# A Strassen feed-forward on one core: eight early pairs in place of four, spills issued by ACT, gate parts three units ahead, down groups of 4, 5 and 6

## The reference, cut to what matters

```
mix = concat([attn, rec]) @ w_out
h = h + rmsnorm(mix, g_post_mix)
u = rmsnorm(h, g_pre_ffn)
f = square(relu(u @ w_ff1)) @ w_ff2        # 1024 -> 4096 -> 1024, 1024 tokens, fp32
h = h + rmsnorm(f, g_post_ffn)
```

## Time and profile before

| | us |
|---|---|
| median of three runs | 2499.36 |
| their range | 2497.77 to 2503.22 |
| the profiled execution | 2501.51 |
| its span, first to last instruction | 2499.5 |
| busy: PE, DVE, ACT, POOL | 2311.5, 1553.2, 1016.2, 557.3 |
| last part of the program: first early unit starts | 1784.8 |
| last down unit starts its last matmul | 2443.9 |

### The profile page before, as it was taken

One profiled execution on the slowest core, in us unless ns is written; L12 is line 12 of the kernel. 1 busy time (PEld: TensorE's weight loads), 2 busy tenths in 40 slices (PEclk: granted clock), 3 DMA queues, 4 the chain that ended last, 5 costly groups with the idle time before them and its releaser, 6 DMA issues. The chain is left out here.

```text
span 2499.5 us, 30965 instructions
## 1 busy us (share of the span) xinstructions
PE 2311.5 (92%) x11293; PEld 1951.4 (78%) x11293; DVE 1553.2 (62%) x2437; ACT 1016.2 (41%) x1688; POOL 557.3 (22%) x467
## 2 busy tenths in 40 slices
PE   8989699989999999999999989789979998899986
PEld 5779588877888888888887988667758887688765
DVE  7699666665643444433444685472898776567787
ACT  5478545453421111111112663474543333454431
POOL 2021222214322222222221211003301221120332
PEclk9975599999999999999999999899989999899998
DMA  9024100014211111111110011002334445553521
GB/s 364 18 85 154 50 14 13 23 44 143 85 34 51 51 51 50 50 37 47 50 50 26 35 34 34 18 1 93 130 123 177 185 169 199 209 185 112 175 68 68
DMA packets 66289, 219.06 MB, mean 88 GB/s; under 512 B 8160, under 2 KB 12416, under 8 KB 63744
## 3 DMA queue, kind: packets, MB, share of 16 engines
q1 hardware_dynamic: 66176, 217.59, 24.9%
HBM read 174.04 MB, written 43.52 MB: 87 GB/s over the span
## 5 line engine op out<-in xcount | busy, mean ns | idle before, releaser
L158 PE MATMUL set<-gate_hi,w_hi 128*128 128x512 f32 x420 | 169.0, 402 | 26.4 <-DVE gate_lo L2329 23.3
L1948 ACT CAST w_hi<-w_raw 128x512 fp32r<-128x512 f32 x152 | 94.4, 622 | 230.0 <-PE set L160 80.3
L1647 POOL TENSOR_TENSOR w_lo<-w_raw,w_hi 128x512 fp32r<-128x512 f32 x64 | 87.3, 1366 | 426.9 <-ACT w_hi L1948 426.8
L158 PE MATMUL set<-b_hi,w_hi 128*128 128x512 f32 x416 | 164.3, 395 | 19.2 <-DVE w_lo L2241 19.2
L159 PE MATMUL set<-gate_lo,w_hi 128*128 128x512 f32 x420 | 167.6, 399 | 0.0
L160 PE MATMUL set<-gate_hi,w_lo 128*128 128x512 f32 x420 | 167.3, 398 | 0.0
L3359 DVE TENSOR_SCALAR work<-work,vec 128x1024 f32<-128x1024 f32 x22 | 17.9, 814 | 236.0 <-ACT work L3089 228.9
L159 PE MATMUL set<-b_lo,w_hi 128*128 128x512 f32 x416 | 163.3, 393 | 0.0
L160 PE MATMUL set<-b_hi,w_lo 128*128 128x512 f32 x416 | 163.3, 393 | 0.0
L3381 DVE SCALAR_TENSOR_TENSOR x<-down,mod,x 128x512 f32<-128x512 f32 x160 | 120.0, 750 | 66.4 <-PE down L160 64.4
L2329 DVE TENSOR_TENSOR gate_lo<-gate_raw,gate_hi 128x512 fp32r<-128x512 f32 x105 | 100.3, 957 | 60.0 <-ACT gate_hi L2006 60.0
(11 more groups left out here) (567 smaller groups left out, 6474.2 us busy)
## 6 DMA issues: line engine op xcount, KB each, us to landing
gates<-x SPq DMA_DIRECT2D x16, 2048.0 KB, 7.3
gate_raw<-gates SPq DMA_DIRECT2D x105, 256.0 KB, 2.8
w_raw<-in_w_ff SPq DMA_DIRECT2D x47, 512.0 KB, 5.9
ada<-in_ada_w SPq DMA_DIRECT2D x32, 512.0 KB, 3.3
work<-in_f_w_u SPq DMA_DIRECT2D x22, 512.0 KB, 3.3
work<-in_f_w_v SPq DMA_DIRECT2D x22, 512.0 KB, 3.4
work<-in_f_w_out SPq DMA_DIRECT2D x22, 512.0 KB, 4.3
down_raw<-in_w_ff SPq DMA_DIRECT2D x18, 512.0 KB, 5.3
```

Of the source, the lines that this page charges most:

```text
L158: nc.tensor.matmul(out, w_hi, x_hi, start=start, stop=False)
L1647: nc.gpsimd.tensor_tensor(lo[:, :], source(n), f32(hi[:, :]), ALU.subtract).then_inc(pool_lo, 1)
L1948: nc.scalar.copy(w_parts(n)[0][:, :], source(n)).then_inc(w_hi_s, 1)
```

## The change

`EARLY` is 8: P1 and P2 of eight pairs are done ahead of the rest. Their results have no room in SBUF all at once beside the squares of h, so SP stores each early P2 to DRAM (`keep_p2`) and loads it straight into block 0 of its gate buffer when that buffer is free (`bring_p2`). The scratch tiles for u2, y and P1 become blocks 5, 7 and 6 of the gate buffer. The store of a gate buffer is issued by ACT (`spill`), as two transfers, 256 KB and 1.5 MB (block 1 is left out for pairs under `LAST`; of pair 15 only four blocks go out, and its block sums are not made). SP no longer waits for block sums. The down groups have 4, 5 and 6 pairs; there are four gate_hi and gate_lo buffers, made three units ahead. DVE's order in the down stage is sum (n+3), gate_lo (n+3), w_lo (n+2). The low parts for the 16th pair are made by DVE instead of POOL. The low parts of raw weights (P1, P2, P4) stay on POOL.

```diff
-EARLY, GROUP = 4, 5
+EARLY = 8
+SIZES = (4, 5, 6)
...
-        raws = raw + [at(f"down_raw{i}", SLOT(i), [P, 2, KT * P]) for i in range(3)]
+        raws = raw + [at(f"down_raw{i}", SLOT(s), [P, 2, KT * P]) for i, s in enumerate((0, 1, 2, 13))]
...
-        early_p = [[work[:, 2 * x + i, 0:512] for i in range(2)] for x in range(EARLY)]
-        u2, y = work[:, 6, 512:1024], work[:, 7, 512:1024]
-        own_p1 = [work[:, 2 + i, 512:1024] for i in range(2)]
+        early_p1 = [work[:, x, 0:512] for x in range(EARLY)]
+        early_p2 = [work[:, x, 512:1024] for x in range(EARLY)]
...
+        EARLY_AT = ((0, 0), (0, 0), (0, 1), (1, 0), (1, 1), (0, 0), (0, 1), (1, 0))
...
+                    if i == P1:
+                        sp.wait_ge(spilled[(w - PAIRS) % 2], 16 * SPILLS * ((w - PAIRS) // 2 + 1))
...
+                def keep_p2(x):
+                    sp.wait_ge(p_s, 2 * x + 2)
+                    sp.dma_start(d["p2_keep"][x], early_p2[x]).then_inc(p2_kept[x], 16)
+
+                def bring_p2(x):
+                    if x >= 2:
+                        sp.wait_ge(spilled[x % 2], 16 * SPILLS * (x // 2))
+                    sp.dma_start(blk(x, 0), d["p2_keep"][x]).then_inc(p2_back[x % 2], 16)
...
+                sp.wait_ge(pool_lo, units.low[9])
+                load_up(1, 1)
+                sp.wait_ge(pool_lo, units.low[11])
+                load_up(0, 0)
+                for x in range(3, 6):
+                    keep_p2(x)
+                sp.wait_ge(pool_lo, units.low[13])
+                load_up(0, 1)
+                sp.wait_ge(pool_lo, units.low[15])
+                load_up(1, 0)
+                for x in range(6, EARLY):
+                    keep_p2(x)
+                sp.wait_ge(kept, 16 * KT)
+                sp.wait_ge(h_squared, N)
+                sp.wait_ge(t_hi_s, 5 * HALF)
+                sp.wait_ge(t_lo_s, 4 * HALF)
+                bring_p2(0)
+                bring_p2(1)
                 for x in range(PAIRS):
                     if x == LAST:
                         sp.wait_ge(done, units.at[(x, P1)] + 1)
-                        for j in (2, 3):
-                            load_down(j, 0)
-                            load_down(j, 1)
+                        load_down(0, 2, 0)
+                        load_down(0, 3, 0)
                         sp.wait_ge(done, units.at[(x, P2)] + 1)
-                        load_down(4, 0)
-                        load_down(4, 1)
                         for b in range(4):
                             load_gate(b)
+                        load_down(0, 2, 1)
+                        load_down(0, 3, 1)
+                        load_down(1, 4, 0)
+                        load_down(1, 4, 1)
                     sp.wait_ge(dve_lo, units.low[units.at[(x, P3)]])
...
-                    sp.wait_ge(t_s, 4 * x + 4)
-                    sp.dma_start(d["gates"][x], gates[x % 2]).then_inc(spilled[x % 2], 16)
-                sp.wait_ge(done, UP)
-                sp.dma_start(end_o_raw[:, 0, :], d["w_ff2"][2 * LAST]).then_inc(end_o_loaded, 16)
-                sp.dma_start(end_o_raw[:, 1, :], d["w_ff2"][2 * LAST + 1]).then_inc(end_o_loaded, 16)
+                    if 1 <= x < EARLY - 1:
+                        bring_p2(x + 1)
...
                 def early_out(n):
+                    x, i = units.all[n]
                     act.wait_ge(done, n + 1)
-                    act.wait_ge(h_added, 7)
-                    nc.scalar.copy(early_p[n // 2][n % 2], bank(n)).then_inc(p_s, 1)
+                    if i == P1:
+                        act.wait_ge(h_added, 7)
+                        nc.scalar.copy(early_p1[x], bank(n)).then_inc(p_s, 1)
+                    else:
+                        act.wait_ge(h_s, h_count(x))
+                        nc.scalar.copy(early_p2[x], bank(n)).then_inc(p_s, 1)
...
                 def square_h(k):
+                    act.wait_ge(p2_kept[k], 16)
                     nc.scalar.activation(work[:, k, span[1]], tok(k, span[1]), ACT.Square).then_inc(h_squared, 1)
 
                 def copy_p1(x):
                     act.wait_ge(done, units.at[(x, P1)] + 1)
-                    act.wait_ge(h_total, 2)
-                    if x >= EARLY + 2:
-                        act.wait_ge(u2_s, x - 1)
-                    nc.scalar.copy(own_p1[x % 2], A_BANK).then_inc(p_s, 1)
+                    act.wait_ge(spilled[x % 2], 16 * SPILLS * (x // 2))
+                    nc.scalar.copy(p1_at(x), A_BANK).then_inc(p_s, 1)
...
+                def spill(x):
+                    if x < LAST:
+                        act.wait_ge(t_s, 4 * x + 4)
+                        act.dma_start(d["gates"][x][:, 0:512], blk(x, 0)).then_inc(spilled[x % 2], 16)
+                        act.dma_start(d["gates"][x][:, 1024:4096], gates[x % 2][:, 1024:4096])\
+                            .then_inc(spilled[x % 2], 16)
...
+                    act.wait_ge(done, UP + b - 3)
+                    nc.scalar.copy(gate_hi[b % 4][:, :], gate_raw[b % 4][:, :]).then_inc(gate_hi_s, 1)
...
+                def out11(x):
+                    if x < EARLY:
+                        dve.wait_ge(p2_back[x % 2], 16 * (x // 2 + 1))
+                        nc.vector.tensor_tensor(blk(x, 0), p1_at(x), blk(x, 0), ALU.add).then_inc(c11_s, 1)
+                    else:
+                        dve.wait_ge(done, units.at[(x, P2)] + 1)
+                        dve.wait_ge(spilled[x % 2], 16 * SPILLS * (x // 2))
+                        dve.wait_ge(p_s, EARLY + x + 1)
+                        nc.vector.tensor_tensor(blk(x, 0), B_BANK, p1_at(x), ALU.add).then_inc(c11_s, 1)
...
+                def end_weights_low(h):
+                    dve.wait_ge(end_o_hi_s, h + 1)
+                    nc.vector.tensor_tensor(end_o_lo[h][:, :], end_o_raw[h], f32(end_o_hi[h][:, :]), ALU.subtract)\
+                        .then_inc(end_o_lo_s, 1)
+
+                def end_gate_low(j):
+                    dve.wait_ge(end_g_hi_s, j + 1)
+                    nc.vector.tensor_tensor(g_lo[j][:, :], end_g_raw[:, j, :], f32(g_hi[j][:, :]), ALU.subtract)\
+                        .then_inc(end_g_lo_s, 1)
...
+                    if n + 2 < UP:
                         if not units.on_pool(n + 2):
                             weights_low(n + 2)
-                        if n + 2 >= UP:
-                            gate_low(n + 2 - UP)
-                    if n + 3 < ALL and not units.on_pool(n + 3):
-                        weights_sum(n + 3)
+                        if n + 3 in units.combined:
+                            weights_sum(n + 3)
+                        if n + 3 == UP:
+                            gate_low(0)
+                    else:
+                        if n + 3 in units.combined:
+                            weights_sum(n + 3)
+                        if n + 3 < ALL:
+                            gate_low(n + 3 - UP)
+                        if n + 2 < ALL and not units.on_pool(n + 2):
+                            weights_low(n + 2)
```

370 lines of the change are left out of this document (199 added, 171 removed).

## The result

The changed kernel takes 2464.8 us (median of 4 runs, 2463.9 to 2466.7) beside 2501.3 (2497.8 to 2503.4) for the kernel before on the same chip: a ratio of 0.9856, interval 0.9839 to 0.9874. The time lies in the predicted range, 15 us above the predicted 2450. One execution of the kernel with four edits (4222.0) and one of before beside it (3286.5) ran far slower than all others of the same kernels, at a lower granted clock, and the ratios leave both out (the median of 2446.5 is 2446.3 without it). The profiled execution has a span of 2461.8; the span fell by 37.7 us, where 50.9 were summed up.

The account below looks back on a forecast made before the run. PE was taken as the bound, interrupted by DVE or what DVE waits for. Gains of 14.0 (up stage), 21.7 (turn) and 15.2 (groups) sum to 50.9, span 2448.6; with 1.5 for small waits 2450 us, range 2439 to 2471.

Parts of the forecast that it names:

- What bounds the kernel: Whole kernel: PE is the bound, interrupted by DVE or what DVE waits for; 24.1, 22.2 and 18.4 us lost at three places.
- Start of the up stage: First up units: PE waits 4.1 us for sum_h(0) and the parts behind it, plus half clock; 7.1 lost instead of 24.1.
- the early units end at 1809.2 + 21.8 = 1831.0: Before the up stage: eight more early units give PE 21.8 us of work, ending at 1831.0.
- Pairs 0 to 7: Up stage: a closed round of spill and fetch takes 14.1 us against PE's 13.6; price 3, bounds 0 and 9.
- Rival 2: Up stage: the spill and fetch round is longer, 17.7 us, costing 22 instead of 3; 2469, 18 %.
- The turn: From up to down stage: earlier gate requests hide the DMA; price 0.5, bounds 0 and 6, 21.7 us gained.
- seven units, 19 us, from there to its use: Down stage: lead of gate 13 behind 5 MB, which take at most 18.3 us; hidden, but by little.
- rival 3: Turn's pause moves to gate 13 or group 2's weights: 5 with its half clock, 8 in all; 2458 to 2462, 12 %.
- The groups: Down stage: new DVE order removes the 0.74 waits and absorbs 2.28 sums; 3.2 lost of 18.4, 15.2 us gained.
- plus six POOL w_lo that lock it out for 1.1 each: Last group's end: POOL's low parts delay DVE, bringing its work to 35.8 us against 32.6 of PE.
- Rival 4: 16th pair on DVE: the end list slips, PE pauses above 3 us twice, final sums start 4 later; 2460, 10 %.
- The other rivals: Besides the summed case (50 %): less cost than charged, 2440, 5 %; slower through copy_p1 waiting for spills, 2500 to 2515, 3 %.

Follow-up runs that it names:

- the kernel with four edits: Changed kernel with sum_h(0) after eight early units, last-group P4 low parts on DVE, x's refill spread, two w_hi ahead of ACT's t4 casts: 2446.5 us, ratio 0.9789.
- the refill spread: Changed kernel with x's eight transfers and two weight loads sent one behind each of gates 12 to 21, not all ahead of gate 13: 2459.6 us, ratio 0.9833.
- the spills on SP: Changed kernel with SP instead of ACT issuing the gate-block spills of pairs 0 to 14: 2468.7 us, ratio 0.9873.

## Why the prediction was right in kind and too high in gain

The figures in brackets are the losses that the prediction left at each place.

**What bounds the kernel**: right. Each of the four pauses is one of PE waiting for DVE, for what DVE holds up, or for what DVE itself waits for. What made the kernel faster is shown in part. Undone one by one, the order and lead of the gate parts cost 9.7 us, the spills on ACT's queue 7.8 and the group sizes nothing. `EARLY` = 4 and the old order of loads at the turn were not put back; that they are behind the 9.1 of the up stage and most of the rest is read from positions.

**Start of the up stage** (7.1 left): the step "the early units end at 1809.2 + 21.8 = 1831.0" failed. They end at 1836.1, by the first pause, 5.9 us. It took POOL's operations beside DVE as a cost to DVE; what a full DVE does to POOL had no price. The text had named the place ("ACT's list there is nearly full"), not priced it. The rest held: sum_h binds, the pause is 4.04 beside 4.1, the half clock 2.6 beside 2.7, h_total released DVE at 1836.9.

**Pairs 0 to 7** (3 left): right in kind, a little high. Spills start at 1867.87, 1881.62, 1895.38, 1909.14, 1922.89 and 1937.83: 13.75 apart (once 14.94), where the round was put at 14.1 and DVE at 13.8. DVE's own 13.8 is what was measured; the round doesn't bind. The 1.5 MB took 5.8, the rest of the spill lay beside it, where 6.4 were taken. Two waits, 0.77 and 1.04, are what came of it, about 2. Rival 2 (the longer round) fell, and the spills on SP showed that one queue would not have brought it either.

**The turn** (0.5 left): the 21.7 came but for 4.1. The price of the transfer held: from 2124.94 the 5 MB and gate 13 took 16.8 us, at most 18.3 were said. What failed is the lead, "seven units, 19 us, from there to its use". On DVE w_lo of the unit before stands behind gate_lo of gate 13, and PE wanted it at 2140.9, 15.9 after the issue. This was rival 3, below its price of 8, and the refill spread shows it.

**The groups** (3.2 left): the small waits are gone as costed, but the fourth pause is 6.8. The step "plus six POOL w_lo that lock it out for 1.1 each", with 1.0 for a wait "at the last P4 unit", failed: in the stretch that made the fourth pause, 2377.96 to 2386.40, DVE was not locked out at all; POOL was, for 8.4 us. (Behind the pause DVE lost some: gate_lo took 1.37 at 2394.14 and 1.78 at 2397.63 instead of 0.69, where no wait of PE above 0.25 came of it.) The rows of before had shown both sides, the join of 3.36 and the 3.02 that PE waited for POOL; only the first was carried over.

So + 5.9 - 0.5 - 1 + 4.1 + 5 = 13.5 of the 50.9, and 37.4 are left; measured are 36.9, and 0.8 more by which this execution reached the stage earlier. That the time lies in the range owes something to the range's width: three steps failed the same way, and no rival had their sum. Rival 4 came in place, a pause above 3 us in the last group, but not in cause. The other rivals didn't come: no copy_p1 made anyone wait, and the final sums start no later.

## What to carry to other kernels

Where two engines hold each other up, as POOL and DVE do here, ask not only how much the slower one delays the faster, but whether the faster one ever stops: beside a list without gaps an operation of 1.29 us took 9.65 at one place and 2.55 at another, so one with a deadline doesn't belong there. A buffer made three units ahead gives its lead only to what stands behind nothing else; count the lead at the first consumer that is queued behind it. And when a pause goes, the next list in program order is what was under it: put each engine's list in the order in which PE needs it, and expect to do it for all of them.
